# A fourth seven-product pair, and three low parts made by the adding DMA, in the first half of the last product

## The reference

```python
    h = rmsnorm(x, a_norm[j])
    y, gate = gmlp_mixer(h, a_w_in[j], a_v_gain[j], a_w_s[j], a_b_s[j])
    w_out = a_w_out[j]
    ...
    x = x + (y * jax.nn.silu(gate)) @ w_out
return rmsnorm(x, final_norm)
```

## Time and profile before

| | us |
|---|---|
| median of 3 runs | 2132.43 (2132.28 to 2132.67) |
| the profiled execution: its own time | 2134.26 |
| its span, first to last instruction | 2132.6 |
| TensorE busy | 2120.7 (99%) |
| VectorE busy | 1758.3 (82%) |
| ScalarE busy | 1389.1 (65%) |
| GpSimd busy | 217.3 (10%) |

### The profile page before, as it was taken

How to read it: one execution, slowest core, us unless ns; L and a number is a source line. 1 busy time by engine, 2 the same in 40 slices (tenths; PEclk the granted TensorE clock), 3 DMA queues, 4 the chain that set the end, 5 groups by cost and what they waited for, 6 DMA issues and landing times.

```text
span 2132.6 us, 30191 instructions
## 1 busy us (share of the span) xinstructions
PE 2120.7 (99%) x10098; PEld 1777.6 (83%) x10098; DVE 1758.3 (82%) x2295; ACT 1389.1 (65%) x1609; POOL 217.3 (10%) x306
## 2 busy tenths in 40 slices
PE   9999999999999999999999999999999999999998
PEld 9988888888888888888888888888888888888886
DVE  5678788675666699899899898988999999998976
ACT  5365455466545677766767667767668777877565
POOL 2021433201000000000000000000000111110000
PEclk9999999999999999999999999999999999999999
DMA  7666555676565688889998887876668888887664
GB/s 258 182 193 208 158 158 150 186 221 174 181 186 185 188 247 251 254 248 250 252 262 244 229 247 226 237 220 197 207 204 238 245 245 244 232 232 228 199 194 139
DMA packets 224192, 458.57 MB, mean 215 GB/s; under 512 B 14584, under 2 KB 14688, under 8 KB 223968
## 3 DMA queue, kind: packets, MB, share of 16 engines
q1 hardware_dynamic: 208608, 402.70, 59.6%
q0 software_dynamic: 14592, 51.46, 13.8%
q10 hardware_dynamic: 896, 3.15, 0.4%
HBM read 409.01 MB, written 3.16 MB: 193 GB/s over the span
## 4 chain that ended last, share of the span: by engine, by line
PE 93%; DVE 4%; issue 2%; ACT 1%; DMA 0%; DVEq 0%; SPq 0%; ACTq 0%
PE gp L2073 33%; PE gp L2141 32%; PE mx L2141 12%; PE gp L2164 7%; PE gp L2168 4%; PE mx L2421 1%; DVE w_lo L1317 1%; PE mx L2305 1%; PE mx L2470 1%; DVE t_lo L1560 0%; DVE t_sum L1539 0%; DVE t_sum L1537 0%; DMA x_tok<-x_in 0%; ACT t_hi L863 0%; PE mx L2121 0%
## 5 line engine op out<-in xcount | busy, mean ns | idle before, releaser
L727 ACT ACTIVATE w_hi<-raw 128x1024 fp32r<-128x1024 f32 x759 | 797.2, 1057 | 540.5 <-PE gp L2073 257.5
L1317 DVE TENSOR_TENSOR w_lo<-raw,w_hi 128x1024 fp32r<-128x1024 f32 x671 | 817.1, 1232 | 229.6 <-ACT w_hi L727 217.6
L2141 PE MATMUL gp<-w_hi,a_hi 128*128 128x512 f32 x617 | 240.5, 390 | 0.0
L2141 PE MATMUL gp<-w_lo,a_hi 128*128 128x512 f32 x617 | 240.1, 389 | 0.0
L2141 PE MATMUL gp<-w_hi,a_lo 128*128 128x512 f32 x617 | 240.0, 389 | 0.0
L2073 PE MATMUL gp<-w_hi,a_hi 128*128 128x512 f32 x576 | 229.9, 399 | 0.0
L2073 PE MATMUL gp<-w_lo,a_hi 128*128 128x512 f32 x576 | 224.6, 390 | 0.0
L2073 PE MATMUL gp<-w_hi,a_lo 128*128 128x512 f32 x576 | 224.3, 389 | 0.0
L1560 DVE TENSOR_TENSOR t_lo<-t_sum,t_hi 128x1536 fp32r<-128x1536 f32 x102 | 178.7, 1752 | 10.4 <-ACT t_hi L863 7.7
L678 POOL DMA_DIRECT2D low<-raw x88 | 74.5, 846 | 1089.9 <-ACT low L734 1089.9
L863 ACT ACTIVATE t_hi<-t_sum 128x1536 fp32r<-128x1536 f32 x102 | 150.8, 1478 | 5.4 <-PE gp L2141 5.4
(11 more groups left out here) (437 smaller groups left out, 4286.0 us busy)
## 6 DMA issues: line engine op xcount, KB each, us to landing
raw<-a_w_in_in SPq DMA_DIRECT2D x192, 512.0 KB, 4.8
raw<-w_ffn_in_in SPq DMA_DIRECT2D x176, 512.0 KB, 5.4
raw<-w_in_in SPq DMA_DIRECT2D x175, 512.0 KB, 3.7
low<-raw POOLq DMA_DIRECT2D x88, 512.0 KB, 6.7
raw<-w_ffn_out_in SPq DMA_DIRECT2D x88, 512.0 KB, 5.5
raw<-a_w_out_in SPq DMA_DIRECT2D x64, 512.0 KB, 4.6
raw<-w_out_in SPq DMA_DIRECT2D x32, 512.0 KB, 4.0
raw<-w_proj_a_in SPq DMA_DIRECT2D x16, 512.0 KB, 3.8
```

The source lines that it names most:

```text
L727: act.activation(w_hi[:, place], raw[:, slot], ACT.Copy).then_inc(hi_ready, 1)
L1317: dve.tensor_tensor(w_lo[:, slot], raw[:, slot], w_hi[:, place], ALU.subtract).then_inc(lo_ready, 1)
L2141: ins = pe.matmul(out_, stat[sp_], mov[mp], start=start and p == 0, stop=stop and p == 2, skip_group_check=True)
```

## The change

`Y_FIRST` gets four seven-product pairs, 4, 6, 9 and 12, instead of 4, 8 and 12, so pairs 6 and 9 are now mixed and 8 is plain. It also joins `BY_DMA` with units 11, 15 and 21, which are the second units of the plain pairs 5, 7 and 10. GpSimd gets the three adding DMAs ahead of the load of `gain_fin`. Nothing ahead of `Y_FIRST` and nothing in `Y_LAST` is changed.

```diff
--- before.py
+++ after.py
@@ -52,9 +52,10 @@
 MIXED_FIRST = (4, 6)
 MIXED_OUT = ((4, 6, 9, 11, 14, 16, 19), (6, 8, 11, 13, 16, 18))
 MIXED_V = (6,)
-MIXED_Y = (4, 8, 12)
+MIXED_Y = (4, 6, 9, 12)
 PLACES = 3
 ADDED = (3, 7, 11, 15)
+ADDED_Y = (11, 15, 21)
 ADDED_OUT = ((11, 15, 21, 25, 31, 35, 41), (7, 11, 15, 21, 25, 31, 35))
 LOWS = 2
 
@@ -505,12 +506,14 @@
                 return 16 * (after(k, i, j) // RAW + 1)
             return i * (16 * S[k].pair // RAW) + 16 * ((unit0[k] + j) // RAW + 1)
 
-        BY_DMA = (FFN_IN, FFN_OUT, UG_IN)
+        BY_DMA = (FFN_IN, FFN_OUT, UG_IN, Y_FIRST)
 
         def added_units(k, i):
 
             if k == FFN_OUT:
                 return ADDED_OUT[i]
+            if k == Y_FIRST:
+                return ADDED_Y
             return tuple(unit for unit in ADDED if i or unit >= RING)
 
         added_from = {}
@@ -705,6 +708,8 @@
                     for unit in added_units(UG_IN, 1):
                         if unit < RING:
                             add_low(UG_IN, 1, unit)
+            for unit in added_units(Y_FIRST, 0):
+                add_low(Y_FIRST, 0, unit)
             pool.wait_ge(unit_used, unit0[Y_FIRST])
             pool.dma_start(gain_fin[:, 0], final_norm.partition_broadcast(P)).then_inc(gain_in, 16)
```

## The result

| | before, us | changed, us |
|---|---|---|
| median of 19 runs | 2132.49 (2132.13 to 2133.84) | 2135.39 (2134.25 to 2137.78) |
| span of the profiled execution | 2132.6 | 2133.4 |
| `Y_FIRST` in it, first matmul to `Y_LAST` | 88.81 | 91.24 |

The account below looks back on a forecast made before the run. TensorE, busy 99% of the span, was taken as the bound. The profiled 2134.26 - 0.68 (matmuls) + 0.78 (pair 6 stall) gave 2134.36 us, on the median 2132.43 + 0.10, 2132.5 us; range 2131.4 to 2134.2.

Parts of the forecast that it names:

- Three matmuls fewer: TensorE in `Y_FIRST`: three matmuls fewer at 0.2267 us each, a gain of 0.68 us.
- Pair 6: TensorE waits at pair 6 for VectorE's `sf_lo` and `t_lo`: 0.78 us lost, bounds nothing and 1.6.
- rival 2: Unit 15's adding DMA lands late, its `low` matmuls wait, up to 1.9 us plus a restart, 2134.5 us; chance 0.15.
- its limit of 7.7 us: At unit 15: the adding DMA may land 7.7 us after issue; each microsecond beyond costs one.
- The Trainium skill's lock between VectorE and GpSimd: VectorE's two-port operations can lock ports GpSimd writes DMA descriptors through, putting unit 15's landing near its slow end.
- GpSimd's queue: `gain_fin` load moves behind unit 21's adding DMA, 1948 to about 2001; costs nothing unless it delays pair 12's raw buffers.
- rival 3: Raw buffers of pair 12 late beside unit 21's addition and `gain_fin`: say 1 us, 2133.5 us; chance 0.05.
- the cover, 7.9 us: Unit 25's raw buffer may take 7.9 us to land before pair 12's sums are late; landings taken as 3.9, at most 6.6.
- The text's own rule: At pair 12: each microsecond the raw buffer lands beyond 7.9 us costs TensorE one.
- The chances: Whole kernel against before: same 0.97, faster 0.01, slower 0.02; 0.2%, 4.3 us, taken as needed to tell a change.
- The range: Whole kernel's time: 2131.4 us, no stall at pair 6 with scatter, to 2134.2, short of rival 2's slow end.

Follow-up runs that it names:

- e10: e1 with seven-product pairs 4, 7, 10, 12 and adding DMAs for units 11 and 27 only; 2132.03 us against 2132.99 before, ratio 0.9996.
- e11: e7 with `y_product` of the last group at step 9 of VectorE's program instead of step 5; 2133.19 us against 2133.33 before, ratio 1.0000.
- e5: The repeat: the changed kernel run once more, nothing altered; 2136.14 us against 2132.71 before, ratio 1.0016.
- e7: e1 without unit 21's adding DMA, so units 11 and 15 only; 2133.58 us against 2132.71 before, ratio 1.0003.
- e1: Changed kernel with `gain_fin` loaded when `Y_FIRST` begins, ahead of the adding DMAs; 2133.22 us against 2133.46 before, ratio 0.9999.
- e2: Changed kernel with the `gain_fin` load held back until TensorE has used unit 24 of `Y_FIRST`; 2133.64 us against 2133.46 before, ratio 1.0001.
- e6: Changed kernel with a second, unused copy of `final_norm` (another megabyte) loaded right behind `gain_fin`; 2138.94 us against 2132.71 before, ratio 1.0024.
- e12: Kernel before, with only the `gain_fin` load held back until TensorE has used unit 16 of `Y_FIRST`; 2132.71 us against 2133.33 before, ratio 0.9997.
- e4: Changed kernel with seven-product pairs 4, 8, 12 as before, keeping its adding DMAs and `gain_fin` behind them; 2133.68 us against 2133.46 before, ratio 1.0001.
- e13: e10 with `y_product` of the last group at step 9 instead of 5; 2133.24 us against 2133.33 before, ratio 0.9999.
- e9: e7 with unit 7 also by adding DMA, so units 7, 11 and 15; 2133.08 us against 2132.99 before, ratio 0.9999.

## Why the prediction was wrong

- *Three matmuls fewer, 0.68 us.* Right: 10098 to 10095, and e10 kept all of it.
- *Pair 6.* Right in mechanism and size: 0.78 us forecast, 0.75 measured, 0.77 in the repeat; e11 shows the cause by taking it away. The forecast had 0.36 + 0.10 at unit 13 and 0.20 + 0.10 at the `t_` products, the trace 0.41 and 0.23, and 0.11 at unit 12, where the text had TensorE arrive with nothing to spare. The rows of `FFN_OUT`, shifted, gave VectorE's whole order: with the 1.65 us by which this execution was early, `sf_sum` came at 1978.63 (forecast 1978.62) and `t_lo` ended at 1987.71 (1987.68).
- *No wait for `low` at unit 15 (rival 2).* Right: the changed kernel's adding DMAs landed in 6.9 to 7.8 us, and its TensorE had no gap ahead of the `low` matmuls. The rival is real in small, and its limit of 7.7 us was right: landings of unit 15's DMA up to 7.6 us cost nothing (e5, e7), 7.8 cost 0.11 us (e1), and 7.9 to 8.7 cost 0.23 to 0.26 (e2, e6, e11). The Trainium skill's lock between VectorE and GpSimd ("SBUF — State Buffer", section "SBUF: two separate sides") did not show: all three issues took 0.86 us, against 0.84 in the earlier trace rows, with VectorE working beside them. Nor did it apply as the prediction used it: it is about two-port operations, and VectorE's here have two inputs from SBUF, which the same section sets apart. Whether VectorE slows the landing itself was not tested.
- *GpSimd's queue and rival 3.* This is the step that failed: the term for late raw buffers of pair 12, which the sum put at nothing. The other terms of the sum came true, and this one measured 2.19 us. The text saw that unit 25's buffer, unit 21's DMA and the megabyte of `gain_fin` are asked for within 2 us, and it gave the cover, 7.9 us (8.8 in the changed kernel's trace, since the token sums, some 1.1 us, need not wait for the buffer). But it set against that the landings of the earlier trace rows, 3.9 and at most 6.6, which are those of buffers with no such company, and gave the case 0.05 and 1 us. The landing was 10.0. Rows with company were at hand: in the kernel before, `FFN_OUT` has raw buffers beside adding DMAs, and there they took up to 9.6 us in 1200 to 1410 us. These are the DMA issues of 1254 to 1262 us:

```profile
raw<-w_ffn_out_in SPq DMA_DIRECT2D x4, 512.0 KB, 7.6
low<-raw POOLq DMA_DIRECT2D x1, 512.0 KB, 7.9
```

- *The same step, after the experiments.* Against a cover of 7.9 us these leave the case about even, before the megabyte is counted; 0.05 was not to be had from them. That the moved load is needed for the loss at unit 23 is shown by e1 and e2, that unit 21's DMA adds to the landing by e7 against e1 (4.7 to 8.2 us) and, with the pairs of before, by e12 against e4 (8.9 to 11.2), and the dose by e6. That such transfers share the same sixteen engines is also what the Trainium skill says ("DMA: Bandwidth & Descriptors", section "Issuing engines are not separate DMA queues"), and the 0.96 of DMA share agrees.
- *The price of a late buffer.* Also missed: VectorE, once late at pair 12, is still late at unit 29 behind the partial results, so the 4.20 us cost TensorE twice, 1.43 and 0.76 us. The text's own rule, one for one beyond 7.9 us, would have given 2.1 us for a landing of 10.0, close to the 2.19; that would have been luck, since by the cover of 8.8 only 1.2 us were due at unit 23, and unit 29 was not in the rule.
- *The chances.* A change of less than 0.2% had 0.97, and the ratio 1.0014 is one, though its interval reaches to 1.0020 and the repeat's to 1.0026. But 2.9 us could be told from no change, where the text had taken 4.3 us to be needed. The range was too narrow above: it ended short of rival 2's slow end, and rival 3's landing was bounded by uncrowded rows.

## What to carry to other kernels

When a step moves on one queue, list the transfers that will be in flight together in its new place, and price each by the landing of rows with the same company: 0.5 MB of addition and 1 MB of load took unit 25's buffer of 0.5 MB from 5.5 to 10.0 us. Ask too when the buffer is asked for: a pair made plain moved that by nine matmuls, 2.0 us. A load with 100 us of freedom goes where nothing waits for its neighbours. And an engine's lateness is not spent where it arises: VectorE's at pair 12 was paid at units 23 and 29, in e13 a wait at 1980 was paid at 2011, and moving 1.2 us of its work (e11) moved the gap with it.

## What the runs showed of the hardware

- A wait of TensorE costs more than the idle time listed for it. At unit 23 of the changed kernel 1.16 us are listed; the matmul started 1.32 us later than at the usual pace (the record of the one before runs on for 0.39 us), and the one behind it 0.11 us more, 1.43 us in all.
- In e6, behind 4.56 us in which TensorE stood, seven matmuls started 0.43 us apart instead of 0.23, which with the ones beside them cost 1.6 us. The granted clock was 0.50 from 2018.9 to 2020.9 us, the lower level, 1.2 GHz, and 1.00, 2.4 GHz, from 2021.3 on; the 0.57 below is a mean over both. Behind the 1.16 us at unit 23 of the changed kernel the pace stayed at 0.23:

```profile
2012.00:2017.00 5.00, 0.67 (x3) 0.21 (x2) 3.63 (x5) 0.92 (x1) 0.00 (x0) 1.00 1.03 392
2017.00:2021.00 4.00, 3.77 (x10) 2.98 (x11) 4.00 (x6) 3.50 (x5) 0.00 (x0) 0.57 0.11 43
2021.00:2026.00 5.00, 5.00 (x24) 4.13 (x23) 5.00 (x6) 3.77 (x6) 0.00 (x0) 1.00 0.48 147
```

- An adding DMA of 512 KB within SBUF landed in 5.6 to 8.8 us in `Y_FIRST` in all runs that had one, where the quickest plain loads of that size took 3.5 to 3.8 us. In e9, where VectorE was waiting for ScalarE, its 1.04 us on ScalarE left only 0.2 of the 1.1 us that it spares VectorE.
- Left open: the times of one kernel spread by 1.7 to 4.6 us in a series, and the arrival at `Y_FIRST` by 2.3 us over the traces. What ahead of it varies was not looked into, nor what the slower executions of the changed kernel lose.
